# State-space turns: the real-power products of the input tables on ScalarE, and the input tables ahead of the output tables

## The reference, cut to what matters

```python
def s5_mixer(u, lam_re, lam_im, log_dt, b_re, b_im, c_re, c_im, d_skip, w_glu):
    dt = jnp.exp(log_dt)[..., None]
    lam_bar = jnp.exp(lam * dt)                     # complex, (2, G, P)
    b_bar = ((lam_bar - 1.0) / lam)[..., None] * b
    for d, rev in ((0, False), (1, True)):
        bu = einsum('bsgc,gpc->bsgp', u, b_bar[d])  # complex
        h_dir = associative_scan(a_l * a_r, a_r * h_l + h_r)   # along the sequence, a = lam_bar[d]
    h = states[0] + states[1]
    y = einsum(h.real, c_re) - einsum(h.imag, c_im) + d_skip * u
    y = gelu(y)
    return y * sigmoid(y @ w_glu)
```

## Time and profile before

| | us |
|---|---|
| median of 3 runs | 3670.86 |
| lowest and highest | 3670.05, 3672.31 |
| time of the profiled execution | 3676.72 |
| its span in the profile | 3674.6 |
| DVE busy, over the whole span | 1171.4 (32%) |
| ACT busy, over the whole span | 763.6 (21%) |
| PE busy, over the whole span | 3384.2 (92%) |

### The profile page before, as it was taken

One profiled execution on the slowest core, in us unless ns is written; L12 is line 12 of the kernel. 1 busy time (PEld: TensorE's weight loads), 2 busy tenths in 40 slices (PEclk: granted clock), 3 DMA queues, 4 the chain that ended last, 5 costly groups with the idle time before them and its releaser, 6 DMA issues.

```text
span 3674.6 us, 40318 instructions
## 1 busy us (share of the span) xinstructions
PE 3384.2 (92%) x15863; PEld 2771.3 (75%) x15863; DVE 1171.4 (32%) x1812; ACT 763.6 (21%) x1366; POOL 1328.4 (36%) x949
## 2 busy tenths in 40 slices
PE   6967679999999999999999999878799999999977
PEld 4855467788887888888888888766677888888866
DVE  5889662533333212000012131365423000012133
ACT  3111261311111212000012130365412000012132
POOL 3320005243334574333336633100053333346643
PEclk8978899999999999999999999989899999999988
DMA  4524414312112332121123334434241211124232
GB/s 180 124 86 128 113 50 166 126 48 55 46 46 86 129 112 81 46 57 46 46 98 137 102 119 149 143 88 114 66 164 58 58 46 46 46 97 160 92 109 92
DMA packets 267614, 344.78 MB, mean 94 GB/s; under 512 B 25335, under 2 KB 209850, under 8 KB 267492
## 3 DMA queue, kind: packets, MB, share of 16 engines
q1 hardware_dynamic: 218968, 240.41, 22.1%
q10 hardware_dynamic: 43564, 85.46, 6.3%
q0 software_dynamic: 4960, 17.22, 1.5%
HBM read 290.18 MB, written 59.15 MB: 95 GB/s over the span
## 4 chain that ended last, share of the span: by engine, by line
PE 81%; DVE 10%; ACT 5%; issue 3%; DMA 1%; POOL 0%; ACTq 0%; DVEq 0%; SPq 0%; POOLq 0%
PE PS L868 73%; PE PS L1957 3%; DVE pl_ab L2067 1%; PE PS L804 1%; DVE pt L737 1%; ACT ph_ab L2004 1%; PE PS L1942 1%; DMA w_raw<-w_up 1%; ACT pr_ab L1994 1%; ACT act L711 1%; ACT act L759 1%; PE PS L422 0%; DVE cs L1523 0%; PE PS L445 0%; DVE oo L1487 0%
## 5 line engine op out<-in xcount | busy, mean ns | idle before, releaser
L277 POOL TENSOR_TENSOR w_lo<-w_raw,w_hi 128x512 fp32r<-128x512 f32 x700 | 938.3, 1372 | 25.1
L273 POOL CAST w_hi<-w_raw 128x2048 fp32r<-128x2048 f32 x175 | 338.7, 1936 | 1683.1 <-DMA w_raw<-ffn_w_gu 608.7
L868 PE MATMUL PS<-h_hi,w_hi 128*128 128x512 f32 x2482 | 802.2, 394 | 20.7 <-DVE h_lo L862 12.0
L868 PE MATMUL PS<-h_lo,w_hi 128*128 128x512 f32 x2482 | 795.1, 391 | 0.0
L868 PE MATMUL PS<-h_hi,w_lo 128*128 128x512 f32 x2482 | 794.8, 391 | 0.0
L868 PEld LDWEIGHTS PS<-h_hi,w_hi 128*128 128x128 f32 x2482 | 468.8, 189 | 120.6 <-DVE h_lo L862 16.3
L868 PEld LDWEIGHTS PS<-h_hi,w_lo 128*128 128x128 f32 x2482 | 468.9, 189 | 98.3
L868 PEld LDWEIGHTS PS<-h_lo,w_hi 128*128 128x128 f32 x2482 | 469.3, 189 | 95.5
L868 PE MATMUL PS<-w_hi,a_hi 128*128 128x512 f32 x1056 | 326.8, 391 | 11.1 <-DVE a_lo L934 7.2
L868 PE MATMUL PS<-w_lo,a_hi 128*128 128x512 f32 x1056 | 326.0, 390 | 0.0
L868 PE MATMUL PS<-w_hi,a_lo 128*128 128x512 f32 x1056 | 325.9, 390 | 0.0
(11 more groups left out here) (307 smaller groups left out, 3348.2 us busy)
## 6 DMA issues: line engine op xcount, KB each, us to landing
w_raw<-ffn_w_gu SPq DMA_DIRECT2D x88, 512.0 KB, 5.0
w_raw<-ffn_w_down SPq DMA_DIRECT2D x88, 512.0 KB, 4.2
w_raw<-w_up SPq DMA_DIRECT2D x44, 512.0 KB, 5.0
w_raw<-w_down SPq DMA_DIRECT2D x44, 512.0 KB, 4.2
xs<-px ACTq DMA_DIRECT2D x40, 512.0 KB, 2.6
w_raw<-w_out SPq DMA_DIRECT2D x32, 512.0 KB, 4.4
w_raw<-w_in SPq DMA_DIRECT2D x28, 512.0 KB, 5.5
px<-xs ACTq DMA_DIRECT2D x7, 2048.0 KB, 10.5
```

Source lines behind the costliest of these rows:

```text
L273: e.tensor_copy(w_hi[b][:, 0:n], w_raw[b][:, 0:n]).then_inc(S("w_hi"), 1)
L277: op = e.tensor_tensor(w_lo[b][:, s], w_raw[b][:, s], w_hi[b][:, s].bitcast(F32), ALU.subtract)
L868: mm = e.matmul(o, a[ai], b[bi], start=start and first, stop=stop and end)
```

## The change

In turns 1 to 5 the products of b with the real part of the powers, which DVE made with two operations for each direction (L1507), are made by ACT in a new function, `g_scaled_act`: for each direction (2), group (4) and power (8) one `activation` with the function Copy and the power's column of `stn` as scale, over 2 x 16 numbers per partition (the real and the imaginary part of b), so 64 instructions a turn. The last one counts up a new semaphore, `ss_x`. DVE still makes the other products into `gy` and adds both; its first sum in each direction now waits for `ss_x`. ACT makes those of turn 1 behind `states(0)`, and those of turn i+2 between `states(i+1)` and `output(i)`. Turn 0 is made as before. In the loop DVE makes the input tables before the output tables, and the waits that guard the shared piece of SBUF change places with them; `ssm_scan` waits for `ss_oo` in place of `ss_g`.

```diff
         def ssm_oo(e, ta, i):
...
                 for k in range(2):
-                    ta.add(e.tensor_tensor(o[:, k, d], r, c[k], ALU.mult))
-                if d:
-                    e.wait_ge(S("ss_oo"), 4 * i + 2)
+                    ta.add(e.tensor_tensor(o[:, k, d], powers(qr, 9, d, i), c[k], ALU.mult))
+                if d or i:
+                    e.wait_ge(S("ss_oo") if d else S("ss_g"), 4 * i + (2 if d else 4))
...
         def ssm_g(e, ta, i):
...
-                for k in range(2):
-                    ta.add(e.tensor_tensor(x[k], r, b[k], ALU.mult))
-                e.wait_ge(S("ss_g") if d else S("ss_oo"), 4 * i + (2 if d else 4))
-                for k in range(2):
-                    ta.add(e.tensor_tensor(gy[:, k], m, b[1 - k], ALU.mult))
+                if i == 0:
+                    for k in range(2):
+                        ta.add(e.tensor_tensor(x[k], powers(qr, CH, d, i), b[k], ALU.mult))
+                if d or i == 0:
+                    e.wait_ge(S("ss_g") if d else S("ss_oo"), 4 * i + (2 if d else 4))
+                for k in range(2):
+                    ta.add(e.tensor_tensor(gy[:, k], powers(qi, CH, d, i), b[1 - k], ALU.mult))
                 ta.settle()
+                if i:
+                    e.wait_ge(S("ss_x"), i)
                 e.tensor_tensor(x[0], x[0], gy[:, 0], ALU.add).then_inc(S("ss_g"), 1)
                 e.tensor_tensor(x[1], gy[:, 1], x[1], ALU.subtract).then_inc(S("ss_g"), 1)
+
+        def g_scaled_act(e, i):
+
+            for d in range(2):
+                q = PRD + 1 if d == 0 else PR
+                for g in range(GSUB):
+                    r = d * G + i * GSUB + g
+                    for k in range(CH):
+                        op = e.activation(gs_[:, :, d, g, k * GC:(k + 1) * GC], bb[:, :, r, :], ACT.Copy, scale=stn[:, q + k, r:r + 1])
+            op.then_inc(S("ss_x"), 1)
...
         def ssm_scan(e, ta, i):
-            e.wait_ge(S("ss_g"), 4 * min(i + 2, TURNS))
+            e.wait_ge(S("ss_oo"), 4 * min(i + 2, TURNS))
...
                 if i + 1 < TURNS:
+                    ssm_g(e, ta, i + 1)
                     ssm_oo(e, ta, i + 1)
-                    ssm_g(e, ta, i + 1)
                 ssm_scan(e, ta, i)
...
             kernel_(0)
             states(0)
+            e.wait_ge(S("ss_dd"), 1)
+            g_scaled_act(e, 1)
             for i in range(TURNS):
                 if i + 1 < TURNS:
                     kernel_(i + 1)
                     states(i + 1)
+                if i + 2 < TURNS:
+                    g_scaled_act(e, i + 2)
                 output(i)
```

More of the change, by code:

```diff
@@ L1474, in rotations_dve, with powers @@
             ta.settle()
+        def powers(q, n, d, i):
+            return st4(q, n, d, i * GSUB).rearrange("p t g -> p g t").unsqueeze(3).to_broadcast([P, GSUB, n, GC])
         def ssm_oo(e, ta, i):
@@ L1480, in ssm_oo @@
             o = oo[i % 2]
+            c = [cc[:, k].rearrange("p (g c) -> p g c", c=GC)[:, g0:g0 + GSUB].unsqueeze(2).to_broadcast([P, GSUB, 9, GC])
+                 for k in range(2)]
             for d in range(2):
                 qr, qi = (PR, PI) if d == 0 else (PRD, PID)
-                r, m = (st4(q, 9, d, g0).rearrange("p t g -> p g t").unsqueeze(3).to_broadcast([P, GSUB, 9, GC]) for q in (qr, qi))
-                c = [cc[:, k].rearrange("p (g c) -> p g c", c=GC)[:, g0:g0 + GSUB].unsqueeze(2).to_broadcast([P, GSUB, 9, GC])
-                     for k in range(2)]
                 for k in range(2):
-                    ta.add(e.tensor_tensor(o[:, k, d], r, c[k], ALU.mult))
-                if d:
-                    e.wait_ge(S("ss_oo"), 4 * i + 2)
+                    ta.add(e.tensor_tensor(o[:, k, d], powers(qr, 9, d, i), c[k], ALU.mult))
+                if d or i:
+                    e.wait_ge(S("ss_oo") if d else S("ss_g"), 4 * i + (2 if d else 4))
                 for k in range(2):
-                    ta.add(e.tensor_tensor(oy[:, k], m, c[1 - k], ALU.mult))
+                    ta.add(e.tensor_tensor(oy[:, k], powers(qi, 9, d, i), c[1 - k], ALU.mult))
                 ta.settle()
@@ L1501, in ssm_g @@
                 qr, qi = (PRD + 1, PID + 1) if d == 0 else (PR, PI)
-                r, m = (st4(q, CH, d, g0).rearrange("p t g -> p g t").unsqueeze(3).to_broadcast([P, GSUB, CH, GC]) for q in (qr, qi))
                 b = [bb[:, k].rearrange("p (d g) c -> p d g c", d=2)[:, d, g0:g0 + GSUB].unsqueeze(2).to_broadcast([P, GSUB, CH, GC])
```

## The result

| | before | changed |
|---|---|---|
| median of 16 runs | 3672.39 us | 3681.01 us |
| lowest to highest | 3669.73 to 3676.63 | 3675.73 to 3690.89 |
| span of the profiled execution | 3674.6 us | 3682.0 us |

The ratio is 1.0026, with a 95% interval of 1.0019 to 1.0033: the change costs about 9.5 us (7 to 12). On the earlier three runs of before, 3670.86, I had forecast 3675, which is 4.3 us more; on the median of 16 runs that would be 3676.7. The time lies inside the range, on the side that I gave 0.38.

A forecast was written before the change was run, and what follows sets the result against it. DVE was taken to bound each 31.57 us turn; waiting for ACT's scalings adds 1.65 us in four turns (+6.6), turn 1's tables save 2.25: +4.3 us on 3670.86, forecast 3675 us, range 3662 to 3687.

The forecast's parts named there:

- What bounds the turn: State-space stretch: DVE sets each 31.57 us turn before; after the change, it waits 3.97 us for ACT's scalings.
- The saving on DVE: Products into gs_ leave DVE in turns 1 to 5: 2.32 us less a turn, 29.25 us if DVE never waited.
- T + 17.01: Moment, in us after the scan's first product (T), when DVE is ready for the first input-table sum.
- One scaling: Distance between starts of two scalings on ACT: 0.213 us, with 64 of them a turn.
- the second rival: ACT's scalings stand 0.243 us apart, as eight small evictions did: +13.8 us, 3685; chance 0.21, plus 0.05 for the extreme.
- Where the scalings start: ACT's first scaling at T + 7.2 us, T being the scan's start, behind kernel_, the transposes and the second gT eviction.
- T + 9.1: Start of ACT's scalings if PE's clock stays low through kernel_ and all transposes, T being the scan's start; chance 0.11.
- Turn 1's tables: Their scalings end at 243.7, DVE asks at 243.63, so nearly the whole saving stays: -2.25 us.
- The end: From scan 4 on no table is made and kernel_(5) fits on PE before turn 4's output: no change.
- ACT fast enough: Scalings under 0.15 us apart end before DVE asks, and all five turns keep 2.32 us: -11.6 us, 3659; chance 0.11.
- Slow rate: Long run of small ACT operations 0.243 us apart, turn 35.1 us: +13.8 us, 3685; chance 0.21, plus 0.05 for the extreme.
- Late transposes: PE's clock still low at the transposes, scalings start 1.9 us later in each of four turns: +12 us, 3683; chance 0.11.

The follow-up runs named there:

- e4: The changed kernel with the number 0.5 in place of the column as scale of the 64 scalings (other values result): 3661.18 us beside 3674.42 before, ratio 0.9961.
- e6: The changed kernel with output tables first and the first direction's scalings made twice, 96 a turn: 3670.69 us beside 3675.28 before, ratio 0.9992.
- e1: The changed kernel with the output tables made ahead of the input tables again, scalings still on ACT: 3661.81 us beside 3674.42 before, ratio 0.9965.
- e5: The changed kernel with PE's transposes ahead of kernel_ and ACT evicting ksb behind the scalings: 3677.11 us beside 3674.53 before, ratio 1.0009.
- e3: The changed kernel with ACT counting after each direction's 32 scalings and DVE waiting per direction: 3668.22 us beside 3674.42 before, ratio 0.998.

## Why the prediction was right, and where it was off

**What bounds the turn.** Right. DVE set it before; in the changed kernel the chain runs through ACT's scalings and back to DVE (from 257 to 292 us they hold 38.5% of it). Of what lies behind the gate's products and up to the end, the net difference is 0.6 us.

**The saving on DVE.** Forecast 2.32 us a turn and a turn of 29.25 for a DVE that doesn't wait; e4 shows 29.27. The places of the waits, T + 17.01 for the first sum and 12.24 us behind it, are 17.00 (273.45 + 1.29 + 0.02, less 257.76, as if nothing were waited for) and 12.26 (278.71 to 290.97) in the changed kernel.

**One scaling.** I took 0.213, from a column Copy of 1024 numbers and from an operation on 4 numbers; it is 0.212. The row of the eight evictions at 0.243, on which the second rival stood, isn't a rule for such runs: 320 scalings keep 0.212, and the 96 in a row in e6 0.213, the wait in between included. Why those eight are 0.243 apart stays open. They alternate between halves of the partitions, which I didn't test.

**Where the scalings start.** T + 7.2 was right in turn 0 (7.20) and turn 2 (7.14), and low in turn 3 (7.51) and above all in turn 1 (9.16). This is the term that was mis-sized. I had kept "PE is up to speed when it comes to the transposes" as the one value for all four turns and T + 9.1 as another case with 0.11; in the run both occur side by side, in one execution. Four times 1.65 should have been between 1.6 and 3.6, turn by turn: 1.64, 3.59, 1.58 and 1.95. Measured +8.77 in place of +6.6.

**Turn 1's tables.** Forecast -2.25, measured -0.35. The same cause one step earlier: the transposes of turn 0, which the change doesn't touch, were at the low clock too. Timelines of PE, before and changed:

```profile
226.93 1.97 PE L1609 MATMUL PS<-ident,gs__171 128*128 128x128 f32 x16
```

```profile
227.13 3.67 PE L1624 MATMUL PS<-ident,gs__171 128*128 128x128 f32 x16
```

So ACT's second eviction came at 230.84 in place of 228.97 and the scalings began at 231.76, 1.9 us late, while DVE happened to be 1.3 us early. It waited 3.25 us, where I had almost none. Its early arrival brought nothing, since it had to wait for ACT. In e1's execution the same transposes took 1.97 us and the same scalings began at 228.92. They took 3.67 in four of the eight profiled executions, so this start is a matter of the execution, and I had taken it as fixed.

**The end.** I had taken everything from scan 4 on as unchanged. It was -2.70 in output(5) and +1.7 later, where PE's clock differs. I had named neither, and neither is shown to come from the change.

With the forecast's own terms the sum is -0.35 + 8.77 - 2.70 + 1.7 = +7.4 us, the difference of the spans, in place of +4.3; the medians differ by 8.6 and the ratio says 9.5. The mechanism and each price but the clock were right. What was off is that I laid the sum on one course of the clock: low through kernel_, high through the transposes, in every turn. Where it stayed low longer, the tables of turn 1 cost 1.9 us more than forecast and turn 1 as much again. The -1.0 at the end takes a part of that back, and this was luck: nothing in the prediction accounts for it.

**The rivals.** ACT fast enough: it would have been so from 0.15 us a scaling on, and e4 with 0.119 shows such a kernel, 13 us below its before where I had given 11.6. Slow rate: refuted. Late transposes: true in one of the four turns, and in the transposes of turn 0, which I hadn't thought of; the windows of PE show it, and e5 and e3 agree.

## What to carry to other kernels

Before work moves from a full engine to an idle one, write down when the idle one can start, how long it takes there, and when the first one asks; the idle share of the engine (ACT was at 11% in a turn) says nothing on that. A table that another engine helps with should be the last that is asked for, and the one made alone should stand in front: the same move was +0.26% in one order and -0.35% in the other. And where a helper delivers in pieces, count the pieces: two counts for two directions made -0.2% out of +0.26%. Both orders were tried in this kernel alone.

## What the runs showed of the hardware

- ACT, 32 numbers a partition, SBUF to SBUF: 0.212 us from start to start with a column as scale and 0.119 with a number, for 64 in a row, the same 13.64 us whether DVE idles beside it for 4 us (changed kernel) or works through (e1). The same 2048 products a partition cost ACT 13.6 us in 64 pieces and DVE 2.4 us in four. By elements alone ACT would need 1.7, an estimate from the 0.83 ns a number that the two widths of the earlier trace rows give.
- PE's clock, after 7.7 to 8.5 us of idle: at the low level when kernel_ begins, in all of turns 1 to 4 of the changed kernel. In turn 2 it was high from the last quarter of kernel_ on, in turn 3 from the transposes on, in turns 1 and 4 it was low through both (transposes of 3.67 us). A chain that goes over PE's first work behind such a pause has a length that changes by 2 us from turn to turn. In e5, which does the waited-for part first, the turns of the profiled execution agree to 0.1 us.
- The idle time alone doesn't settle the level. Behind 3.19 us of idle the first products of output(5) ran at the low clock, behind 3.34 us (e1) they reached the high one within the first pair.
